# A fused block on one Trainium2 core: six more FFN pairs as seven half products, with part of the splitting and a norm's scale and shift moved to GpSimd

## What is computed

```
x = layer_norm_2(ALPHA * x + gt1 * mix, ln1_g[l], ln1_b[l])
h = x * (1.0 + sc2) + sh2
gu = h @ w_ffn_in[l]                      # 1024 -> 2 * 2816
f = (jax.nn.silu(gu[..., :FFN_HIDDEN]) * gu[..., FFN_HIDDEN:]) @ w_ffn_out[l]
x = layer_norm_2(ALPHA * x + gt2 * f, ln2_g[l], ln2_b[l])
```

## Time and profile before

| | |
|---|---|
| median of 3 runs | 1573.38 us (1569.16 to 1573.64) |
| profiled execution | 1572.88 us, its span 1570.8 us |
| granted TensorE clock, mean | 0.995 of full speed |
| busy: TensorE | 1518.1 us (97%) |
| busy: VectorE | 1093.5 us (70%) |
| busy: ScalarE | 749.5 us (48%) |
| busy: GpSimd | 191.9 us (12%) |
| FFN input products, pairs 1 to 21 | 1227.3 to 1443.7 us |

### The profile page before, as it was taken

How to read it: one execution, slowest core, us unless ns; L and a number is a source line. 1 busy time by engine, 2 the same in 40 slices (tenths; PEclk the granted TensorE clock), 3 DMA queues, 4 the chain that set the end, 5 groups by cost and what they waited for, 6 DMA issues and landing times.

```text
span 1570.8 us, 25892 instructions
## 1 busy us (share of the span) xinstructions
PE 1518.1 (97%) x10408; PEld 1252.6 (80%) x10408; DVE 1093.5 (70%) x1898; ACT 749.5 (48%) x1253; POOL 191.9 (12%) x159
## 2 busy tenths in 40 slices
PE   7999999999999999999999999988898999999998
PEld 6878786888888877777788888767767899989886
DVE  5999994666655478758544747886547978867556
ACT  5544455535522477747632625654424544444223
POOL 2435364500010000000004000000000000000000
PEclk9999999999999999999999999999999999999999
DMA  6323243454465323232424232210002233433331
GB/s 220 94 86 120 90 147 108 160 165 146 147 184 182 116 86 95 90 111 81 147 95 142 74 121 81 81 43 4 3 29 86 90 108 106 123 97 121 101 98 54
DMA packets 45798, 166.18 MB, mean 106 GB/s; under 512 B 5280, under 2 KB 5408, under 8 KB 45680
## 3 DMA queue, kind: packets, MB, share of 16 engines
q1 hardware_dynamic: 43056, 155.95, 30.8%
q0 software_dynamic: 2624, 8.59, 1.9%
HBM read 162.42 MB, written 2.10 MB: 105 GB/s over the span
## 4 chain that ended last, share of the span: by engine, by line
PE 79%; DVE 15%; ACT 3%; issue 2%; DMA 0%; SPq 0%; DVEq 0%; ACTq 0%
PE bank L643 24%; PE bank L645 24%; PE bank L644 23%; DVE bank L2390 7%; PE bank L1366 1%; PE bank L1218 1%; ACT scratch L654 1%; DVE small L2416 1%; DVE x_rows L2390 1%; PE bank L1197 1%; DVE scratch L2387 0%; DVE weight_lo L699 0%; PE bank L1463 0%; ACT weight_hi L691 0%; DMA x_in<-in_x 0%
## 5 line engine op out<-in xcount | busy, mean ns | idle before, releaser
L691 ACT ACTIVATE weight_hi<-raw 128x1024 fp32r<-128x1024 f32 x195 | 205.8, 1057 | 384.6 <-PE bank L645 381.1
L643 PE MATMUL bank<-h_T_hi,weight_hi 128*128 128x512 f32 (+1 forms) x848 | 342.0, 403 | 2.8 <-DVE conv_in L2387 2.1
L699 DVE TENSOR_TENSOR weight_lo<-raw,weight_hi 128x1024 fp32r<-128x1024 f32 x138 | 168.8, 1224 | 238.6 <-ACT weight_hi L691 238.6
L645 PE MATMUL bank<-h_T_hi,weight_lo 128*128 128x512 f32 (+1 forms) x848 | 329.8, 389 | 0.0
L644 PE MATMUL bank<-h_T_lo,weight_hi 128*128 128x512 f32 (+1 forms) x848 | 329.2, 388 | 0.0
L643 PEld LDWEIGHTS bank<-h_T_hi,weight_hi 128*128 128x128 f32 x848 | 160.1, 189 | 43.2 <-issue 8.5
L2390 DVE SCALAR_TENSOR_TENSOR bank<-conv_in,columns,bank 128x512 f32<-128x512 f32 x240 | 181.4, 756 | 8.3
L644 PEld LDWEIGHTS bank<-h_T_lo,weight_hi 128*128 128x128 f32 x848 | 160.3, 189 | 33.5 <-issue 3.6
L645 PEld LDWEIGHTS bank<-h_T_hi,weight_lo 128*128 128x128 f32 x848 | 159.8, 188 | 33.8
L699 POOL TENSOR_TENSOR weight_lo<-raw,weight_hi 128x1024 fp32r<-128x1024 f32 x57 | 141.8, 2488 | 154.1 <-ACT weight_hi L691 154.1
L643 PE MATMUL bank<-h_T_hi,half_weight_hi 128*128 128x256 f32 (+1 forms) x240 | 79.1, 330 | 0.0
(11 more groups left out here) (500 smaller groups left out, 3193.0 us busy)
## 6 DMA issues: line engine op xcount, KB each, us to landing
raw<-in_weights SPq DMA_DIRECT2D x289, 512.0 KB, 3.5
x_in<-in_x SPq DMA_DIRECT2D x4, 512.0 KB, 5.8
x_rows<-in_x POOLq DMA_DIRECT2D x4, 512.0 KB, 4.9
out<-x_rows SPq DMA_DIRECT2D x3, 512.0 KB, 2.6
mem_in<-in_mem POOLq DMA_DIRECT2D x2, 512.0 KB, 4.2
ln_rows<-in_ln_g POOLq DMA_DIRECT2D x4, 256.0 KB, 4.4
ln_rows<-in_ln_b POOLq DMA_DIRECT2D x4, 256.0 KB, 5.1
silu_row<-in_c POOLq DMA_DIRECT2D x1, 512.0 KB, 6.6
```

What stands on the lines that cost most here:

```text
L643: pe.matmul(o, lhs[0], rhs[0], start=start, stop=False, skip_group_check=onto)
L645: return pe.matmul(o, lhs[1], rhs[0], start=False, stop=stop, skip_group_check=onto)
L691: act.activation(weight_parts(u)[0][:, :], raw[u % RAW][:, :], ACT.Copy).then_inc(*weight_hi.up(u))
L699: engine.tensor_tensor(lo[:, :], raw[u % RAW][:, :], view(hi[:, :]), ALU.subtract).then_inc(*ready.up(u))
```

## The change

`SEVENS` now holds all pairs from 2 to 20; only 1 and 21 stay whole. In every seven pair the lower parts of `B11`, `B21` and `B22` are made by GpSimd (`POOL_PARTS`), with a semaphore of their own (`part_lo_pool`), those of the four `T` parts by VectorE as before. The scale and shift of the rows go from VectorE to GpSimd: one tile of rows (four operations of 128x512) behind the parts of each of the pairs 5, 8, 11 and 14. The rows of the last norm are loaded by GpSimd at pair 16, in place of behind the last shift.

```diff
-SEVENS = tuple(n for n in range(2, FT) if n % 3)
+SEVENS = tuple(range(2, FT - 1))
+POOL_PARTS = ("B11", "B21", "B22")
+GAINS_AT = (5, 8, 11, 14)
+LAST_ROWS_AT = 16
...
         norm_rows("ln1")
-        pool.wait_ge(*moved.at("ln1", TT - 1, 1))
-        norm_rows("ln2")
+        for n in SEVENS:
+            for part in POOL_PARTS:
+                rest_of_part(pool, n, part, part_lo_pool)
+            if n in GAINS_AT:
+                pool.wait_ge(*rows_loaded.at("ln1", 1, 1))
+                t = GAINS_AT.index(n)
+                for half in range(2):
+                    rows_half = x_rows[t][:, cut(half, 512)]
+                    pool.tensor_tensor(rows_half, rows_half, ln_rows[half][:, :], ALU.mult).then_inc(*pool_own.up())
+                    pool.wait_ge(*pool_own.last())
+                    pool.tensor_tensor(rows_half, rows_half, ln_rows[2 + half][:, :], ALU.add).then_inc(*gained.up(t, half))
+            if n == LAST_ROWS_AT:
+                pool.wait_ge(*gained.at(TT - 1, 1))
+                norm_rows("ln2")
...
+    def part_ready(n, part):
+        return part_lo_pool.at(n, part) if n in SEVENS and part in POOL_PARTS else part_lo.at(n, part)
+
+    def rest_of_part(engine, n, part, ready):
+        hi, lo = half_of(n, part)
+        engine.wait_ge(*part_hi.at(n, part))
+        engine.tensor_tensor(lo, part_source(n, part), view(hi), ALU.subtract).then_inc(*ready.up(n, part))
...
             for part in parts_of(n)[first:last]:
-                dve_part(dve, n, part)
+                if n not in SEVENS or part not in POOL_PARTS:
+                    rest_of_part(dve, n, part, part_lo)
...
         added("C22", up[:, lasts], third_sum, "T1")
-        if n + 1 not in SEVENS and n > SEVENS[0]:
-            dve_gains(dve)
...
         feed_lo(dve, FT)
+        dve.wait_ge(*gained.at(TT - 1, 1))
         dve.wait_ge(*rows_loaded.at("ln2", 1, 1))
```

More of the change, by code:

```diff
@@ L628, in build @@
     weight_summed, part_hi, part_lo = signal("weight_summed"), signal("part_hi"), signal("part_lo")
+    part_lo_pool = signal("part_lo_pool")
     used, seven_act, seven_dve = signal("part_used"), signal("seven_act"), signal("seven_dve")
     gate_taken = signal("whole_gate_taken")
-    moved = signal("residual_moved")
+    moved, gained = signal("residual_moved"), signal("rows_gained")
     progress = {}
@@ L636, in start_pass @@
     def start_pass():
-        progress.update(hi=0, lo=0, gains=0)
+        progress.update(hi=0, lo=0)
         table[0] = None
@@ L745, in sync_program @@
                         sp.wait_ge(*weight_summed.at(n, "T4"))
-                        sp.wait_ge(*part_lo.at(n, "B21" if label == "ffn_g" else "B22"))
+                        sp.wait_ge(*part_ready(n, "B21" if label == "ffn_g" else "B22"))
                     else:
@@ L1602, in pe_whole @@
                 hi, lo = half_of(n, part)
-                pe.wait_ge(*part_lo.at(n, part))
+                pe.wait_ge(*part_ready(n, part))
                 for j in range(KT // 2):
@@ L3106, in dve_sum @@
         dve_rest(dve, sums[name][1][:, :, :], full_sums[name][:, :, :], sums[name][0][:, :, :], sum_hi.at(name)).then_inc(*sum_lo.up(name))
-    def dve_part(dve, n, part):
-        hi, lo = half_of(n, part)
-        dve_rest(dve, lo, part_source(n, part), hi, part_hi.at(n, part)).then_inc(*part_lo.up(n, part))
     def dve_parts(dve, n, first, last):
@@ L3129, in dve_weight_sum @@
         dve.tensor_tensor(weight_sums[name][:, :], a, b, ALU.subtract).then_inc(*weight_summed.up(n, name))
[L3131 to L3136, removed]
     def dve_whole(dve, n):
@@ L3213, in dve_ffn @@
         dve_sum(dve, "S4")
-        dve.wait_ge(*rows_loaded.at("ln1", 1, 1))
         for n in range(1, FT):
```

## The result

The changed kernel takes 1617.98 us (median of 6 runs, 1616.82 to 1621.04) against 1572.29 (6 runs, 1569.16 to 1573.64): the ratio is 1.0295, with a 95% interval of 1.0282 to 1.0309. It is slower by 45.7 us. The prediction was 1608, slower, in a range of 1585 to 1624. The profiled execution took 1618.42 us, with a span of 1616.7.

The account below looks back on a forecast made before the run. VectorE, held by GpSimd's reads, was to replace TensorE as the bound. Terms -10.1 + 36 + 2 + 15 - 2 gave +41, with GpSimd under bank additions +24; +35 was taken, giving 1608 us, range 1585 to 1624.

Parts of the forecast that it names:

- The bound: Input products' stage: VectorE at 10.7 to 11.5 us a pair passes TensorE's 9.52 and becomes the bound.
- The first rival: No exclusion in this loop: VectorE has 8.2 us a pair, all parts in time, about 1564 us; chance 0.09.
- The price of an operation: A GpSimd subtraction between two VectorE two-input operations costs VectorE 1.11 us, or 0.83 under a bank addition.
- a hold to the letter: Shared read interface held for whole instructions: 1.40 us an operation instead of 1.11, sum some 20 us higher.
- the second rival: A shorter hold: GpSimd's subtraction holds VectorE for less than its length, between 1574 and 1591 us; chance 0.13.
- The alternating sum: GpSimd's subtractions come between VectorE's two-input operations: 11.5 us a pair, 36 us over 18 preparations, +41 in all.
- the one with GpSimd under bank additions: GpSimd gets in only under VectorE's bank additions: 10.7 us a pair, 21 us over 18 preparations, +24 in all.
- +35: Loss in us taken between the sums of +41 and +24, giving a time of 1608 us.
- The runs of rows: Rows' scale and shift, 16 GpSimd operations behind pairs 5, 8, 11 and 14: 18 or 13 us, 15 taken.
- The gate rows: Ahead of pair 18: 2.8 us of TensorE time before now falls into waits, -2.
- The wait of 1.0 us: VectorE waits 1.0 us each seven pair for ScalarE's upper part, and this stays when VectorE has less to do.
- The third rival: Worse than the sum: 1.42 us an operation gives 8 more, a falling clock adds; chance 0.06 of over 1624.

Follow-up runs that it names:

- experiment 3: Kernel before plus three unused GpSimd operations in each of pairs 3 to 20: two-input subtractions 1595.78 us, fills 1571.8, one-input multiplications 1576.98.
- experiment 1: Changed kernel with all lower parts and the rows' scale and shift back on VectorE, 19 seven pairs kept: 1593.98 us, ratio 1.013.
- experiment 2: Changed kernel with only the rows' scale and shift back on VectorE: 1615.21 us, ratio 1.0267.
- experiment 5: Changed kernel with the gate rows' four matmuls and ScalarE's copies one pair later, ahead of pair 19: 1613.66 us, ratio 1.0273.
- experiment 4: ScalarE's T4 upper part and first silu put ahead of the second silu: changed kernel 1601.47 us, experiment 1's kernel 1573.54, kernel before 1571.89.

## Why the prediction was right, and where its terms were off

*The bound.* The prediction said that VectorE takes the lead through GpSimd's reads. Experiments 3 and 1 show it: 54 such GpSimd operations with nothing taken from VectorE cost 23.5 us, and with all of GpSimd's operations given back to VectorE the changed kernel gains 24. (That the two numbers are so close is chance: the first is in a kernel with eight whole pairs, the second includes the work that VectorE gets back.) The first rival, no exclusion, is out.

*The price of an operation.* 1.11 us was worked out from one product of 1024 columns held for 2.84 us and the line through 2.44 and 0.46 us. Measured: 1.10 (1.78 - 0.68), not the 1.40 of a hold to the letter, and 1.257 to 1.272 us for GpSimd's subtraction alone, under both estimates, 1.31 and 1.41. The shorter hold, the second rival, rested on a one-input operation; experiment 3 shows that such a one does hold for 0.41 only, but this loop has none. So that row was no evidence for it.

*The choice between the sums.* The alternating sum gave 11.5 us a pair and +41, the one with GpSimd under bank additions +24, and I took +35 since "five additions and the wait of 1.0 in each pair must catch some of it". They catch one operation in three. The last two upper parts of one pair and the first of the next become ready close together on ScalarE; so GpSimd's three operations run in one piece of 4.7 us. The first starts at 1340.76, under the last addition of the pair (1340.54), and costs 0.83, as the prediction has it for such a one; the other two stand beside `hidden` and the first weight sums, where VectorE has no addition, cost 1.10 each, and are over before the next additions begin. A pair is 11.41 us. The chain of who releases GpSimd's operations (ScalarE's last parts) would have told their place. These terms came to +34.0, where the alternating sum had 36.

*The sum.* The stage lost 44.5 us, 3.5 more than the alternating sum: -2.0 in the pairs, -0.6 in pair 2, +0.4 in the runs, +6.5 in the gate rows, -0.8 in the pairs behind them. The further 6 us by which +35 lies under +41 were a guess at what the additions and the wait would catch, and no more than 2.0 of them was caught. So the mechanism and its price were right, and that the time still fell into the range, 6 us under its end, owes something to the width of the range.

*The runs of rows.* 15 predicted, 15.4 measured; experiment 2 gives back only 2.9 of it, because on VectorE the same four operations cost 2.7 to 3.8 us a run.

*The gate rows* are the one term whose mechanism was wrong: "The gate rows ahead of pair 18, 2.8 us of TensorE time before, now fall into waits: -2". Measured +4.5. TensorE's time for them is indeed no loss where it would wait anyway, but TensorE doesn't only work there, it waits for VectorE's diagonals, and VectorE is now late. In order, the wait falls on TensorE after the last product of pair 17, and what VectorE then needs from pair 18 starts later: VectorE, the bound, stands still for 4.95 us. Experiment 1 has this too, without GpSimd (pair 17 15.57 us beside 9.67 for pair 16, with a wait of 2.62 us for the diagonals), so the hold is not needed for it; experiment 5 moves the place and gives 4.1 us back. The hold adds 2.0 us to the diagonals (3.68 against 1.65).

*The wait of 1.0 us.* The prediction had it in the loop (8.2 = 7.05 + 1.0 + 0.1), rightly: with experiment 4's order VectorE's waits for upper parts of `half_weight` fall from 18.4 to 1.8 us in the stage, and the time falls by 16.5. It isn't even: plain pairs go from 11.4 to about 10.0 us, pairs with a run only from 15.3 to 15.6 to 14.5 to 15.0. In the kernel before the wait lies beside TensorE's work and is worth nothing.

*What was called right or wrong in advance.* TensorE's busy share of the stage is 227.7 of 262, 87% (80 to 85 was said); pairs 11.4 (10.5 to 11.5) and 15.3 to 15.6 with a run (13 to 15, a little short); VectorE's held operations 1.78, additions 0.41, GpSimd 1.26 alone to 1.82. The third rival had a higher price of an operation (not seen) and a clock that falls: it fell, and what it cost is in the last section.

## What to carry to other kernels

Before work is moved from VectorE to GpSimd, take the ratio of the two prices from the trace: here a subtraction of 0.60 us on VectorE cost VectorE 1.10 us when GpSimd made it, so the move loses even though GpSimd is idle. By the prices of experiment 3 an operation that reads nothing (no cost) or one tile (0.41 us) would be the better one to move, and so would one that meets VectorE's additions from PSUM, which were never held; no run here moved such work. When the bound changes its engine, go once through every step that waits for the new bound (small ones such as the gate rows too), since what was hidden is now waited for in the order of the program. And where two kinds of step alternate, one that needs VectorE and one that spares it, numbers between the ends are worth a run: with ScalarE's new order four whole pairs took 1565.27 us, eight 1571.89 and two 1573.54. The run with four also has the rows and the gate rows beside whole pairs, so how much of its lead over the one with two is the number and how much the place isn't shown.

## What the runs showed of the hardware that was not expected

A VectorE TENSOR_SCALAR with one SBUF tile and one column (128x128) is held by GpSimd's subtraction as well. The eight diagonals take 1.65 us in all in the kernel before and in experiment 1, with no GpSimd operation beside them, and 3.68 here beside two. Over the whole program, with minimum, median and maximum:

```profile
L3082 DVE TENSOR_SCALAR scratch<-ident,mod x16: 269/277/1297, 1149.9 to 1443.3; 128x128 f32<-128x128 f32 x16
```

2.03 more is two operations held for 1.02 each. In experiment 5, with three of GpSimd's beside them, they take 4.80, 3.15 more. The Trainium skill, "SBUF — State Buffer", section "Who interferes with whom", lists `tensor_scalar` among the operations that can enter a two-port mode and then contend with GpSimd; the row agrees that it can be held (1.297 against 0.277 us), in which mode it ran no run here shows, and the prediction had counted only operations of two tiles.

The granted clock was 1.00 in the stage before. Now it falls in some of the pairs (0.95 over the stage), though a pair is only 1.9 us longer than TensorE needs. The windows of pairs 3 and 4:

```profile
1253.00:1264.40 11.40, 10.92 (x85) 10.66 (x84) 10.26 (x15) 4.83 (x11) 4.56 (x3) 0.91 0.31 94
1264.40:1275.80 11.40, 10.40 (x84) 10.00 (x84) 10.26 (x15) 4.82 (x11) 4.69 (x3) 1.00 0.32 93
```

In pair 3 TensorE spends a part of the time at 1.2 GHz, the lower of its two levels, and has more busy time (10.92 against 10.40), yet both pairs take 11.40 us: as long as VectorE leads, the slower stretch is paid from TensorE's waits. At the gate rows there is nothing to pay it from, since VectorE waits for TensorE there. Two matmuls take 2.05 us at a granted clock of 0.50, where they take 1.02 at 1.00 in experiment 5.
